# Expert routing with one wide decode per head, its product and half of the one-hot rows on GpSimd

## The reference, cut to what matters

```python
q = (hb @ w_pq).reshape(TOK_BLOCK, PEER_HEADS, 2, PEER_DHALF)
s = jnp.einsum('thpd,hpnd->thpn', q, sub_keys)
s1, i1 = lax.top_k(s[:, :, 0], 16)
s2, i2 = lax.top_k(s[:, :, 1], 16)
cand_s = s1[..., :, None] + s2[..., None, :]      # 16 x 16 sums
top_s, pos = lax.top_k(cand_s, 16)
idx = take(i1 * 128 + i2, pos)                    # 16 experts per head
gate = softmax(top_s)
act = gelu(einsum(expert_u[idx], hb))
out = einsum(gate * act, expert_v[idx])
```

## Time and profile before

| what | us |
|---|---|
| median of 3 runs | 2305.17 (2304.72 to 2308.77) |
| profiled execution, its own time | 2299.01 |
| its span | 2297.2 |
| TensorE busy | 2176.3 |
| VectorE busy | 1500.9 |
| ScalarE busy | 995.1 |
| GpSimd busy | 21.5 |

### The profile page before, as it was taken

One profiled execution on the slowest core, in us unless ns is written; L12 is line 12 of the kernel. 1 busy time (PEld: TensorE's weight loads), 2 busy tenths in 40 slices (PEclk: granted clock), 3 DMA queues, 4 the chain that ended last, 5 costly groups with the idle time before them and its releaser, 6 DMA issues.

```text
span 2297.2 us, 42480 instructions
## 1 busy us (share of the span) xinstructions
PE 2176.3 (95%) x15408; PEld 1952.7 (85%) x15408; DVE 1500.9 (65%) x2932; ACT 995.1 (43%) x1618; POOL 21.5 (1%) x32
## 2 busy tenths in 40 slices
PE   7999999899999998999898879969999999999998
PEld 6998997799889976899887647859888999999997
DVE  4556997555645546655675556989987666666665
ACT  4434765433533345533451343224434444444443
POOL 0000000000000000000000000000000000000000
PEclk9999999999999999999999999989999999999999
DMA  5554653355475534455431014433477666665654
GB/s 195 181 184 156 214 188 129 131 189 187 143 283 184 197 115 135 149 186 187 157 101 32 19 56 138 147 101 136 165 235 235 207 221 204 207 186 187 183 188 132
DMA packets 107231, 377.28 MB, mean 164 GB/s; under 512 B 11697, under 2 KB 17601, under 8 KB 106753
## 3 DMA queue, kind: packets, MB, share of 16 engines
q1 hardware_dynamic: 102528, 354.88, 47.3%
q0 software_dynamic: 4608, 21.15, 3.0%
HBM read 362.29 MB, written 13.69 MB: 164 GB/s over the span
## 4 chain that ended last, share of the span: by engine, by line
PE 82%; DVE 9%; ACT 3%; DVEq 2%; DMA 2%; issue 1%; ACTq 1%; SPq 0%
PE bank L341 67%; PE bank L367 4%; PE bank L1522 3%; PE bank L2406 3%; DMA ring<-in_w 1%; ACTq L464 1%; DVE arena L2523 1%; DVE arena L2530 1%; DVE arena L2524 1%; DVE w_lo L298 1%; ACT w_hi L293 1%; PE bank L556 1%; PE bank L323 1%; DVE arena L2559 0%; PE bank L325 0%
## 5 line engine op out<-in xcount | busy, mean ns | idle before, releaser
L298 DVE TENSOR_TENSOR w_lo<-ring,w_hi 128x1024 fp32r<-128x1024 f32 x581 | 703.0, 1224 | 425.1 <-ACT w_hi L293 423.4
L293 ACT ACTIVATE w_hi<-ring 128x1024 fp32r<-128x1024 f32 x581 | 605.4, 1056 | 637.0 <-PE bank L341 553.8
L341 PE MATMUL bank<-u_hi,w_hi 128*128 128x256 f32 x2568 | 730.2, 284 | 7.8 <-DVE w_lo L298 7.8
L341 PE MATMUL bank<-u_hi,w_lo 128*128 128x256 f32 x2568 | 728.0, 284 | 0.0
L341 PE MATMUL bank<-u_lo,w_hi 128*128 128x256 f32 x2568 | 728.0, 283 | 0.0
L341 PEld LDWEIGHTS bank<-u_hi,w_hi 128*128 128x128 f32 x2568 | 493.5, 192 | 19.0 <-DVE w_lo L298 8.3
L341 PEld LDWEIGHTS bank<-u_lo,w_hi 128*128 128x128 f32 x2568 | 493.6, 192 | 7.4 <-issue 0.5
L341 PEld LDWEIGHTS bank<-u_hi,w_lo 128*128 128x128 f32 x2568 | 493.6, 192 | 0.0
L341 PE MATMUL bank<-w_hi,x_hi 128*128 128x512 f32 x992 | 390.0, 393 | 9.0 <-DVE x_lo L1027 4.0
L341 PE MATMUL bank<-w_lo,x_hi 128*128 128x512 f32 x992 | 388.6, 392 | 0.0
L341 PE MATMUL bank<-w_hi,x_lo 128*128 128x512 f32 x992 | 386.5, 390 | 0.0
(11 more groups left out here) (310 smaller groups left out, 1732.4 us busy)
## 6 DMA issues: line engine op xcount, KB each, us to landing
ring<-in_w SPq DMA_DIRECT2D x264, 512.0 KB, 3.7
ring<-in_expert_u SPq DMA_DIRECT2D x128, 512.0 KB, 3.5
ring<-in_expert_v SPq DMA_DIRECT2D x128, 512.0 KB, 4.1
ring<-in_ssm_in SPq DMA_DIRECT2D x40, 512.0 KB, 4.5
gate_dram<-con SPq DMA_DIRECT2D x16, 576.0 KB, 2.8
arena<-gate_dram POOLq DMA_DIRECT2D x9, 1024.0 KB, 8.7
ring<-in_ssm_out SPq DMA_DIRECT2D x16, 512.0 KB, 3.5
ring<-in_w_o SPq DMA_DIRECT2D x16, 512.0 KB, 4.2
```

Of the source, the lines that this page charges most:

```text
L293: act.activation(w_hi[slot][:, :], ring[slot][:, :], ACT.Copy).then_inc(hi_made[slot], 1)
L298: dve.tensor_tensor(w_lo[slot][:, :], ring[slot][:, :], w_hi[slot][:, :].bitcast(F32), ALU.subtract).then_inc(freed[slot], 1)
L341: mm = pe.matmul(out, left[a], right[b], start=start and n == 0, stop=stop and n == 2, skip_group_check=True)
```

## The change

On VectorE the two halves of the decode become one: rows of `score`, `top` and `pick` are arranged half by half (2 x 2 = 4 rows of 16), `cand` is one addition of 512, the comparison one of 1024 elements. The product of `pick` with `top_f` moves to GpSimd (1024 elements, once per head, in place), and the sum (`sums`, 1024 elements) is taken one head later, between the additions and the second search; for the last head it follows at once. VectorE waits for GpSimd's product of head i-1 before it overwrites `top_f`.

For each one-hot set GpSimd makes rows 0 and 1 of `one_a` and VectorE rows 2 and 3 (SCALED); TensorE waits for both. Three gate tiles precede the turn and two follow it; the other eleven stand after sets spread evenly (after set 2, then every 5 or 6). In the last head ScalarE evicts two u tiles and two gate tiles before it waits for the gates' exponential.

In `ffn2` VectorE evicts all four quarters. Semaphores of two small loads and of the quarters are merged, and VectorE's wait on the fourth quarter in `attn` is dropped.

```diff
@@ -512,8 +512,6 @@
-            if s == "attn":
-                dve.wait_ge(S("kv_turned"), 4)
             rows(0)
@@ -599,7 +597,7 @@
             if q >= 2:
-                pe.wait_ge(S(("kv_rows", "kv_cols")[q % 2]), 1)
+                pe.wait_ge(S("kv_made"), q - 1)
             for c in range(4):
@@ -681,13 +679,6 @@
             silu(1, FC // 2 - 1)
-            if stage_of(k) == HOLDS_KV:
-                for q in (1, 3):
-                    act.wait_ge(S("kv_turned"), q + 1)
-                    for c in range(4):
-                        ins = act.activation(quarter(u_t, q)[:, c, :], TP[1][:, c * P:(c + 1) * P], ACT.Identity,
-                                             scale=V("g_kv", 4 + c, 5 + c))
-                    ins.then_inc(S("kv_cols"), 1)
@@ -717,10 +708,10 @@
             if stage == HOLDS_KV:
-                for q in (0, 2):
+                for q in range(4):
                     dve.wait_ge(S("kv_turned"), q + 1)
-                    dve.tensor_tensor(quarter(u_t, q), TP[0][:, :].rearrange("p (c t) -> p c t", c=4),
-                                      spread(V("g_kv", 0, 4), P), ALU.mult).then_inc(S("kv_rows"), 1)
+                    dve.tensor_tensor(quarter(u_t, q), TP[q % 2][:, :].rearrange("p (c t) -> p c t", c=4),
+                                      spread(V("g_kv", 4 * (q % 2), 4 * (q % 2) + 4), P), ALU.mult).then_inc(S("kv_made"), 1)
             lead_next(dve, stage)
@@ -2243,7 +2233,7 @@
-        TG, SETS = 4, 4
+        TG, SETS, SCALED = 4, 4, 2
         peer_area = KEPT * T
@@ -2257,8 +2247,8 @@
         GATE_U = PRE - ROUTE_PRE
-        UNDER_TURN = 3
-        TILE_AFTER = {5 * t + 1: UNDER_TURN + t for t in range(GATE_U - UNDER_TURN)}
+        AT_CHOICE, UNDER_TURN = 3, 5
+        TILE_AFTER = {T // TG * t // (GATE_U - UNDER_TURN) + 2: UNDER_TURN + t for t in range(GATE_U - UNDER_TURN)}
         V_SLOTS = (1, 3, 0, 2)
@@ -2276,9 +2266,10 @@
         best, best_i, best_a, best_b, best_af, best_bf, gate = (area(9216 + 32 * n, TT, TOPK) for n in range(7))
+        best_ab, best_abf = area(9280, 2 * TT * TOPK), area(9344, 2 * TT * TOPK)
         gate_sum = area(9472, 2, TT)
-        pick = area(9728, TT, TOPK, TOPK)
-        choice = area(10240, 3, TT, P)
+        pick = area(9728, 2 * TT, TOPK, TOPK)
+        choice = area(10752, 3, TT, P)
         gates_of = area(0, KEPT, T)
@@ -2355,7 +2346,7 @@
                     for n in range(2):
-                        at = (2 * tt + n) * P
+                        at = (TT * n + tt) * P
                         mm = pe.matmul(ROT[2][:, at:at + P], pq_t[:, n, tt * P:(tt + 1) * P],
@@ -2372,18 +2363,18 @@
-            pe.wait_ge(S("keys_loaded"), 16)
+            pe.wait_ge(S("table_loaded"), 32)
             queries(0)
...
                 head(i, more=i < PH - 1)
-            gate_tile(0)
-            gate_tile(1)
+            for g in range(AT_CHOICE):
+                gate_tile(g)
             pe.wait_ge(S("choice_ready"), 1)
...
             mm.then_inc(S("choice_turned"), 1)
-            for g in range(2, UNDER_TURN):
+            for g in range(AT_CHOICE, UNDER_TURN):
                 gate_tile(g)
@@ -2401,6 +2392,7 @@
                 pe.wait_ge(S("one_hot"), token + (SETS + 1) * TG)
+                pe.wait_ge(S("pool_rows"), PH + k + 1)
                 pe.wait_ge(S("gates_out"), token + TG)
@@ -2433,10 +2425,17 @@
                     queries(i + 1)
+                else:
+                    tiles(i)
+                    for g in range(AT_CHOICE - 1):
+                        gate_tile(g)
                 act.wait_ge(S("best_ready"), i + 1)
...
                     scores(i + 1)
+                    tiles(i)
+
+            def tiles(i):
                 for n in range(2):
@@ -2469,7 +2468,7 @@
             act.preload_act_table(ACT.Gelu)
-            for g in range(UNDER_TURN):
+            for g in range(AT_CHOICE - 1, UNDER_TURN):
                 gate_tile(g)
@@ -2500,6 +2499,19 @@
         def peer_pool(pool):
+            for i in range(PH):
+                pool.wait_ge(S("picks_found"), i + 1)
+                pool.tensor_tensor(pick, pick, top_f.unsqueeze(2).broadcast_to([P, 2 * TT, TOPK, TOPK]),
+                                   ALU.mult).then_inc(S("pool_rows"), 1)
+            pool.wait_ge(S("choice_ready"), 2)
+            for k in range(T // TG):
+                g, token = k % SETS, TG * k
+                pool.wait_ge(S("gates_done"), token + TG)
+                for t in range(SCALED):
+                    at = token + t
+                    ins = pool.tensor_scalar(one_a[:, g, t, :], C("iota"), choice_t[:, 0, at:at + 1], choice_t[:, 2, at:at + 1],
+                                             ALU.is_equal, ALU.mult)
+                ins.then_inc(S("pool_rows"), 1)
             for s in range(2):
@@ -2530,34 +2542,31 @@
+            def sums(i):
+                of_head = slice(TOPK * i, TOPK * (i + 1))
+                dve.reduce_sum(choice.rearrange("p n t k -> p (n t) k")[:, 0:2 * TT, of_head], pick, AX.X)
+
             for i in range(PH):
...
                 top16(top, top_i, score, score2, range(4))
+                if i:
+                    dve.wait_ge(S("pool_rows"), i)
                 dve.tensor_copy(flat(top_f), as_int(flat(top_i)))
-                for tt in range(TT):
-                    dve.tensor_tensor(cand[:, tt, :].rearrange("p (a b) -> p a b", a=TOPK), spread(top[:, 2 * tt, :], TOPK),
-                                      top[:, 2 * tt + 1, :].unsqueeze(1).broadcast_to([P, TOPK, TOPK]), ALU.add)
+                dve.tensor_tensor(cand.rearrange("p t (a b) -> p t a b", a=TOPK), top[:, 0:TT, :].unsqueeze(3).broadcast_to([P, TT, TOPK, TOPK]),
+                                  top[:, TT:2 * TT, :].unsqueeze(2).broadcast_to([P, TT, TOPK, TOPK]), ALU.add)
+                if i:
+                    sums(i - 1)
                 dve.drain()
...
                 dve.drain()
-                dve.tensor_copy(flat(best_af), as_int(flat(best_a)))
-                dve.tensor_copy(flat(best_bf), as_int(flat(best_b)))
-                dve.drain()
-                for n, at in enumerate((best_af, best_bf)):
-                    for tt in range(TT):
-                        dve.tensor_tensor(pick[:, tt, :, :], spread(at[:, tt, :], TOPK),
-                                          C("iota", 0, TOPK).unsqueeze(1).broadcast_to([P, TOPK, TOPK]), ALU.is_equal)
-                    dve.drain()
-                    for tt in range(TT):
-                        dve.tensor_tensor(pick[:, tt, :, :], pick[:, tt, :, :],
-                                          top_f[:, 2 * tt + n, :].unsqueeze(1).broadcast_to([P, TOPK, TOPK]), ALU.mult)
-                    dve.drain()
-                    dve.reduce_sum(choice[:, n, :, of_head], pick, AX.X)
-                    dve.drain()
+                dve.tensor_copy(best_abf, as_int(best_ab))
+                dve.drain()
+                dve.tensor_tensor(pick.rearrange("p r k a -> p (r k) a"), spread(best_abf, TOPK),
+                                  C("iota", 0, TOPK).unsqueeze(1).broadcast_to([P, 2 * TT * TOPK, TOPK]), ALU.is_equal).then_inc(S("picks_found"), 1)
                 dve.wait_ge(S("gate_exp"), i + 1)
@@ -2565,6 +2574,9 @@
                 dve.drain()
+            dve.wait_ge(S("pool_rows"), PH)
+            sums(PH - 1)
+            dve.drain()
             dve.sem_inc(S("choice_ready"), 1)
@@ -2604,7 +2616,7 @@
                                   spread(choice_t[:, 1, token:token + TG], NKEYS), ALU.is_equal)
-                for t in range(TG):
+                for t in range(SCALED, TG):
                     at = token + t
```

More of the change, by code:

```diff
@@ L623, in ffn_sync @@
                 sp.wait_ge(S("h_updated"), 4 * upd[HOLDS_KV] + 1)
-                sp.dma_start(rel[0:BUCKETS, :], io["rel_bias"]).then_inc(S("rel_loaded"), 16)
+                sp.dma_start(rel[0:BUCKETS, :], io["rel_bias"]).then_inc(S("table_loaded"), 16)
             with sp.Fori(0, FC // 2 - 1) as i:
@@ L647, in ffn_tensor @@
             if stage == HOLDS_KV:
-                pe.wait_ge(S("rel_loaded"), 16)
+                pe.wait_ge(S("table_loaded"), 16)
                 pe.wait_ge(S("rest_loaded"), 16)
@@ L1123, in kv_tensor @@
         def kv_tensor(pe):
-            pe.wait_ge(S("kv_rows"), 2)
-            pe.wait_ge(S("kv_cols"), 2)
+            pe.wait_ge(S("kv_made"), 4)
             arrived(pe, 2, "kv")
@@ L2314, in peer_sync @@
             sp.wait_ge(S("h_updated"), 4 * upd["peer"] + 1)
-            sp.dma_start(keys_all.rearrange("p (h n) -> p h n", h=PH), io["keys"].rearrange("h p n -> p h n")).then_inc(S("keys_loaded"), 16)
+            sp.dma_start(keys_all.rearrange("p (h n) -> p h n", h=PH), io["keys"].rearrange("h p n -> p h n")).then_inc(S("table_loaded"), 16)
             with sp.Fori(0, PH - 1) as i:
```

## The result

The change is slower: 2315.46 us in the median of 11 runs (2311.39 to 2325.9) against 2306.36 us of the kernel before in 11 runs (2303.73 to 2310.54). The ratio is 1.0045, 95% interval 1.0033 to 1.0056: +9.1 us where -11.9 us had been forecast, and above the range's upper end of 2308.

The account below looks back on a forecast made before the run. VectorE was taken to set the pace of the one-hot stretch by 3%, with routing near TensorE's beat. Decode -6.6 and one-hot stretch -5.3 made -11.9 us, 2305.2 to 2293.3 us; range 2279 to 2308.

Parts of the forecast that it names:

- The decode: Routing: heads of 16.15 us on VectorE with the product on GpSimd, decode done at 1543.7, -6.6 us.
- the held product: Routing, each head: VectorE's product of the gates waits 1.7 us while GpSimd's product holds the shared port.
- The first rival: Routing: VectorE and GpSimd do not disturb each other, heads at TensorE's 14.7 us, together -24.7, 2280.5 us; chance 0.28.
- The one-hot stretch: Sets and gate tiles from the transposes on: TensorE the pace, 105.7 us against 110.98, -5.3 us.
- The condition beside it: One-hot stretch: the -5.3 us holds only if a set comes every 1.49 us.
- The slower rival: One-hot stretch: GpSimd's two rows cost 1.0, added to VectorE's 1.12 a set; total +22.3, 2327.5 us; chance 0.14.
- The break-even: One-hot stretch: from 0.73 us for GpSimd's pair of rows on, the kernel is slower by more than 0.2%.
- Keys and values: Keys and values, ffn2's end: VectorE's two more operations of 0.69 us cost 0, at worst 0.6.

## Why the prediction was wrong

*The decode: right.* A head of 16.15 us was forecast and is 16.22 (GpSimd's products start at 1432.23 and 1545.76, 113.53/7); the held product was put at 1.7 and is 1.89; GpSimd's product at 2.1 and is 2.35; decode done 6.6 us earlier was forecast, 7.2 measured. The Trainium skill's figure ("GPSIMD Engine Reference", section 3.1), by which 2.3 was an estimate, was nearer to the 2.35. That VectorE and GpSimd disturb each other there, and by what, was shown twice, by moving the gates' product away and by moving GpSimd's. The first rival (no disturbance) is out. The reason that the forecast gave from its rows for taking the hold was a weak one: it spoke of one-input TENSOR_SCALAR operations, while what was held is a product with two inputs.

*The one-hot stretch: wrong, and it alone.* The step that failed is "GpSimd's two rows need 0.26 by the memset's rate, 1.0 if a row is three streams of 128 and 0.1; I take 0.32". They need 1.94 (1.54 at rest). A memset of bf16 was no price for a comparison with a multiplication: a row has 0.33 us of its own and 3.4 ns per element, where I had 0.03 and 1.0. So the upper bound was too low as well, and with it the range. The condition beside it ("provided a set comes every 1.49 us") was right: in the run with one row it is met, and the sets took 105.6 us against the 105.7 worked out.

The 1.94 has two parts, and it takes both for the loss. With the pair at 1.54, the 60 sets behind the four of lead would need 92.4 us, inside the 95.2 that TensorE has for them: no loss. That is an estimate, since no run had two rows unhindered; with rows of 0.91 the sets took 120.9. The hold-up, 128 x 0.20 = 26 us, is near the 22 by which the change's sets exceed those of the run with one row. It could cost this only because a row at 0.77 leaves no room for it.

*The slower rival: the right outcome by the wrong sum.* It added VectorE's and GpSimd's time; at the true 1.94 it would have given 200 us for the stretch (64 x (1.12 + 1.94) + 4.2). It took 128, GpSimd's 124 and the start. VectorE is hardly held by the rows (its comparison takes 0.69 us beside most of them, 0.82 at most); GpSimd is. Exclusion did not make the two add up here; it made the dearer of the two dearer, from 0.77 to 0.97 a row. The rule of the Trainium skill that the forecast cited there ("SBUF — State Buffer", section "SBUF: two separate sides"), the loser of the lock blocked for the whole instruction, the trace bears out for a row that starts inside a comparison, and not for a comparison that starts inside a row; the last section has the numbers. The break-even that I put at 0.73 for the pair (the point from which the kernel is slower by 4.6 us) was therefore too low. By these runs it lies near (110.98 + 7.2 + 4.6 - 4.2)/64 = 1.85, and no change at all near 1.78: estimates.

*Keys and values, tiles:* 0 was forecast for the first. No run tried it alone, but the table's two stretches give the medians without it, to within 1 us in the change. The tiles' move cost some 2 us where VectorE is the pace; that it is a gain where TensorE is, one tile of 3.46 less behind the transposes, is worked out and was not tried alone.

## What to carry to other kernels

Price an operation on GpSimd from a row of the same operation, per instruction and per element; where no row has it, take a bound several times VectorE's time (here 3 times its 0.255 at rest, 4 times beside it), and see which share still fits under the pace. With one row of four the kernel gained 12 us, with two it lost 9; all of that difference lies in the sets (-5.0 against +17.2). Put behind the start of a GpSimd operation only what reads one tensor: the same instructions in another order were worth 9.5 us. And where a wait has two counters, look at which engine has no idle time, not at the name that the profile gives.

## What the hardware showed that was not expected

GpSimd's rows and VectorE's sets ran in lockstep: 1.10 us per row beside sets of 1.11, 1.38 beside sets of 1.37, and 1.1 even for half a row, although a row takes 0.77 alone. What decides is where a row starts. Of the change's 128 rows, those that start inside a comparison are held for what is left of it: 1.38 us for one that starts 0.07 us into it, 1.26 at 0.18, 1.13 at 0.32, 1.00 at 0.45, and 0.96 at its end. So a row that comes late starts later in the next comparison and is held less, and the two fall into step. The 24 rows that start shortly ahead of a comparison, while none runs, keep their 0.79 us:

```profile
1578.85 0.79 POOL L2512 TENSOR_SCALAR arena<-con,arena 128x128 f32<-128x128 f32 x1
1579.01 0.82 DVE L2617 TENSOR_TENSOR arena<-con,arena 128x512 f32<-128x512 f32 x1 [0.40 <-PE bank L2398]
```

The comparison is held by a row in 9 cases only, all like this one: it starts 0.16 us into the row and takes 0.82 us instead of 0.69. From 0.29 us into a row on it takes its 0.69. So GpSimd's short row stands in the comparison's way only in its first 0.3 us, while the comparison stands in a row's way for its whole length. GpSimd's long product in turn held a two-input operation of VectorE for its whole rest. VectorE's one-input rows held GpSimd too, by 0.05 to 0.3 us; why they do was not tried further.
